# Two post-norms by column chunk, gate rows made ahead of them, and a feed-forward block that begins with its first group

## The reference

```python
def rms_norm_2(x, g):
    y = xf * lax.rsqrt(jnp.mean(xf * xf, axis=-1, keepdims=True) + EPS)
    return (y * g.astype(jnp.float32)).astype(x.dtype)
...
mod = jax.nn.silu(c) @ w_mod[l] + b_mod[l]
sh_m, sc_m, ga_m, sh_f, sc_f, ga_f = [m[:, None, :] for m in jnp.split(mod, N_MOD, axis=-1)]
...
y = gated_merge(y_c, y_h, p_gc, p_gh, w_out[l])
x = x + ga_m * rms_norm_2(y, norm_post_mix[l])
h2 = modulate(rms_norm_2(x, norm_pre_mlp[l]), sh_f, sc_f)
x = x + ga_f * rms_norm_2(sq_relu_mlp(h2, mlp_w1[l], mlp_w2[l]), norm_post_mlp[l])
```

## Time and profile before

| | us |
| --- | --- |
| median of 3 runs | 2971.78 |
| lowest and highest | 2967.68, 2972.05 |
| the profiled execution | 2973.79 |
| span of its trace | 2972.0 |
| PE busy in it | 2857.4 |
| DVE busy | 2014.7 |
| ACT busy | 1355.9 |

### The profile page before, as it was taken

One profiled execution on the slowest core, in us unless ns is written; L12 is line 12 of the kernel. 1 busy time (PEld: TensorE's weight loads), 2 busy tenths in 40 slices (PEclk: granted clock), 3 DMA queues, 4 the chain that ended last, 5 costly groups with the idle time before them and its releaser, 6 DMA issues.

```text
span 2972.0 us, 34985 instructions
## 1 busy us (share of the span) xinstructions
PE 2857.4 (96%) x13258; PEld 2370.4 (80%) x13258; DVE 2014.7 (68%) x2263; ACT 1355.9 (46%) x1633; POOL 146.9 (5%) x103
## 2 busy tenths in 40 slices
PE   7998999999999999999999999989979999999997
PEld 6786787888888887787788888888857888888886
DVE  4665779799789787776686487575557754544554
ACT  4446354444443454555444444653434444344442
POOL 0100001010010100000000000000000001010000
PEclk9999999999999999999999999999989999999998
DMA  7661878987878988555666666405547876665653
GB/s 227 198 195 51 277 255 282 320 266 271 286 258 285 324 287 276 177 184 177 202 184 193 194 188 182 131 1 184 190 144 241 275 220 185 193 189 191 188 188 120
DMA packets 322668, 622.52 MB, mean 209 GB/s; under 512 B 27415, under 2 KB 29591, under 8 KB 320919
## 3 DMA queue, kind: packets, MB, share of 16 engines
q1 hardware_dynamic: 319015, 597.96, 63.1%
q10 hardware_dynamic: 3504, 22.55, 2.0%
HBM read 614.14 MB, written 7.24 MB: 209 GB/s over the span
## 4 chain that ended last, share of the span: by engine, by line
PE 83%; DVE 9%; issue 3%; DMA 3%; ACT 2%; SPq 0%; DVEq 0%; POOL 0%; ACTq 0%; POOLq 0%
PE ps L1281 77%; DVE macc L1930 3%; DVE wlo L1741 2%; DMA raw<-w_in 2%; PE ps L1386 1%; PE ps L1256 1%; ACT whi L648 1%; PE ps L1428 1%; PE ps L1646 1%; DVE tcol L2051 1%; PE ps L1628 1%; PE ps L1608 1%; DMA raw<-w_up 0%; DMA raw<-w_o 0%; PE ps L1357 0%
## 5 line engine op out<-in xcount | busy, mean ns | idle before, releaser
L1741 DVE TENSOR_TENSOR wlo<-raw,whi 128x1024 fp32r<-128x1024 f32 x940 | 1171.9, 1252 | 812.0 <-ACT whi L648 807.5
L648 ACT ACTIVATE whi<-raw 128x1024 fp32r<-128x1024 f32 x940 | 995.8, 1060 | 1312.1 <-PE ps L1281 1222.1
L1281 PE MATMUL ps<-whi,hhi 128*128 128x512 f32 x2064 | 811.7, 393 | 1.7 <-DVE hlo L2057 1.2
L1281 PE MATMUL ps<-whi,hlo 128*128 128x512 f32 x2064 | 804.7, 390 | 0.0
L1281 PE MATMUL ps<-wlo,hhi 128*128 128x512 f32 x2064 | 804.3, 390 | 0.0
L1281 PE MATMUL ps<-whi,xhi 128*128 128x512 f32 x1632 | 649.6, 398 | 21.0 <-DVE wlo L1741 16.4
L1281 PE MATMUL ps<-wlo,xhi 128*128 128x512 f32 x1632 | 642.2, 393 | 0.0
L1281 PE MATMUL ps<-whi,xlo 128*128 128x512 f32 x1632 | 641.8, 393 | 0.0
L1281 PEld LDWEIGHTS ps<-whi,hhi 128*128 128x128 f32 x2064 | 388.2, 188 | 83.4 <-DVE hlo L2057 3.1
L1281 PEld LDWEIGHTS ps<-whi,hlo 128*128 128x128 f32 x2064 | 388.0, 188 | 81.6
L1281 PEld LDWEIGHTS ps<-wlo,hhi 128*128 128x128 f32 x2064 | 388.3, 188 | 79.5 <-issue 1.0
(11 more groups left out here) (280 smaller groups left out, 1548.0 us busy)
## 6 DMA issues: line engine op xcount, KB each, us to landing
raw<-w_in SPq DMA_DIRECT2D x296, 512.0 KB, 4.3
raw<-mlp_w SPq DMA_DIRECT2D x256, 512.0 KB, 3.7
mraw<-w_mod SPq DMA_DIRECT2D x192, 512.0 KB, 6.1
raw<-w_up SPq DMA_DIRECT2D x128, 512.0 KB, 5.1
raw<-w_down SPq DMA_DIRECT2D x128, 512.0 KB, 5.3
raw<-w_o SPq DMA_DIRECT2D x32, 512.0 KB, 5.8
raw<-w_ple_gate SPq DMA_DIRECT2D x32, 512.0 KB, 4.2
raw<-w_out SPq DMA_DIRECT2D x32, 512.0 KB, 4.3
```

The source lines that it names most:

```text
L648: nc.scalar.activation(whi[:, s % NSLOT], raw[:, s % NSLOT], ACT.Copy).then_inc(hi_done, 1)
L1281: ins = nc.tensor.matmul(ps[:, bank(par) + th], a[:, kt, th * P:(th + 1) * P], b[:, (s + u) % NSLOT, k], start=(kt == 0 and m == 0), stop= ...
L1741: nc.vector.tensor_tensor(wlo[:, s % NSLOT], raw[:, s % NSLOT], whi[:, s % NSLOT].bitcast(F32), ALU.subtract)\
```

## The change

- `post3` goes by chunk. ACT squares each chunk of `wo2` out of PSUM instead of copying it, DVE multiplies it by the gate row into `yrow`, and after the last one DVE adds the four chunks to `res` while ACT squares them for `norm4`.
- The gate row of `post3` is made in the stage `pw`, in four parts of 512, in banks 6 and 7; that of `post4` in chunks 18 and 19 of `mlp2`. ACT copies each part out.
- PE begins `mlp2` when the first group is ready; groups 2 to 7 are transposed ahead of pieces 0 to 5 of its first chunk.
- The last part of the modulation work moves from chunks 0 to 7 of `mlp2` to chunks 8 to 15.
- `post4` goes by chunk: three of the four result chunks are squared and multiplied during the chunk after them. SP sends each chunk of `res`, 512 KB, as it is finished.

The core of the diff:

```diff
@@ both @@
-                    ("mlp1", "sbbb", 16, (4,) * 8), ("mlp1", "sssss", 24, (5,) * 8), ("mlp2", "ssss", 0, (4,) * 8)]
+                    ("mlp1", "sbbb", 16, (4,) * 8), ("mlp1", "sssss", 24, (5,) * 8), ("mlp2", "ssss", 8, (4,) * 8)]
@@ SP @@
             mlp("mlp2", w_up2, w_down2)
+            for c in range(4):
+                cs = slice(c * NCH, (c + 1) * NCH)
+                sp.wait_ge(S["res", "post4"], c + 1)
+                sp.dma_start(rows_of(out[0])[:, :, cs], res[:, :, cs]).then_inc(out_done, 16)
+            sp.wait_ge(out_done, 64)
@@ ACT @@
+            def gate_row_out(n, j, dst):
+                act.wait_ge(gb_done, 4 * n + j + 1)
+                nc.scalar.activation(dst[:, j * NCH:(j + 1) * NCH], ps[:, 6 + j % 2], ACT.Copy).then_inc(gb_out, 1)
...
+                        10: lambda: gate_row_out(0, 0, gbc), 11: lambda: gate_row_out(0, 1, gbc),
+                        14: lambda: gate_row_out(0, 2, gbc), 15: lambda: gate_row_out(0, 3, gbc)}
...
-                chunk(p0 + 8 * c, evac_to(yrow, c * NCH, g0 + c), extra=slots(wo_slots, 8 * c))
...
-            postnorm_gated("post3", 0, yrow, lambda e: e.wait_ge(acc_free, plan["mlp2"][1] + 2))
-            norm_mod("norm4", res, lambda e: e.wait_ge(S["res", "post3"], 2))
-            mlp("mlp2", 16, False, {})
-            postnorm_gated("post4", 1, yrow, lambda e: e.wait_ge(acc_free, plan["end"][1] + 2))
-            for th in range(TH):
-                act.wait_ge(S["res", "post4"], 2)
-                act.dma_start(rows_of(out[0])[:, th], res[:, th]).then_inc(out_done, 16)
-            act.wait_ge(out_done, 32)
+                chunk(p0 + 8 * c, lambda c=c, g=g0 + c: psum_squares("post3", c, g), extra=slots(wo_slots, 8 * c))
+            for c in range(4):
+                res_squares("norm4", "post3", ojunk, c)
+            first_row("norm4")
...
+            last = 8 * (len(SEQ) * NSB - 4)
+            mlp("mlp2", 16, False, place({**{g: (lambda g=g: mod_high("norm4", g, xhi)) for g in range(8)},
+                                          **{146 + 4 * j: (lambda j=j: gate_row_out(1, j, gbc4)) for j in range(4)},
+                                          **{last + 8 * c + 10: (lambda c=c: post4_squares(c)) for c in range(3)}}))
+            post4_squares(3)
@@ PE @@
+            def gate_row(n, k, j):
+                pe.wait_ge(mcol_done, k + 1)
+                if n == 0 and j % 2 == 0:
+                    pe.wait_ge(oc_done, NPAIR)
+                if 4 * n + j >= 2:
+                    pe.wait_ge(gb_out, 4 * n + j - 1)
+                for b in range(4):
+                    kt = 4 * j + b
+                    ins = nc.tensor.matmul(ps[:, 6 + j % 2, b * P:(b + 1) * P], mcol[:, k, kt:kt + 1].to_broadcast([P, P]),
+                                           ident, start=True, stop=True)
+                ins.then_inc(gb_done, 1)
...
-            gate_rows(3, plan["mlp2"][1])
-            norm("norm4")
-            pe.wait_ge(x_lo, 24)
-            mlp("mlp2", 16, {})
-            gate_rows(4, plan["end"][1])
+            pe.wait_ge(S["xn", "norm4"], 1)
+            pe.wait_ge(S["xm", "norm4"], 1)
+            norm_turn("norm4", 0, xs)
+            norm_turn("norm4", 1, xs)
+
+            def mlp2_part(u):
+                if u + 2 < 8:
+                    norm_turn("norm4", u + 2, xs)
+                pe.wait_ge(x_lo, 16 + u + 1)
+            mlp("mlp2", 16, place({**{u: (lambda u=u: mlp2_part(u)) for u in range(8)},
+                                   **{144 + 4 * j: (lambda j=j: gate_row(1, 4, j)) for j in range(4)}}))
@@ DVE @@
             for c in range(4):
-                chunk(plan["wo2"][0] + 8 * c, extra=slots(wo_slots, 8 * c))
...
+                chunk(p0 + 8 * c, lambda c=c, g=g0 + c: psum_gain("post3", c, g), extra=slots(wo_slots, 8 * c))
             dve.wait_ge(reload, 16)
-            postnorm("post3", yrow, lambda e: e.wait_ge(acc_free, plan["mlp2"][1] + 2))
-            norm_mod("norm4", res, lambda e: e.wait_ge(S["res", "post3"], 2), mcol[:, 2], modT[:, 3 * KT:4 * KT, 0])
-            mlp("mlp2", {})
+            for c in range(4):
+                dve.wait_ge(acc_free, g0 + c + 3)
+                post_res("post3", yrow, c)
+            chunk_mean_square("norm4", SQ)
+            dve.wait_ge(S["res", "post3"], 4)
+            scaled_row("norm4", res, xs)
...
+            mlp("mlp2", place({0: lambda: [col4(0), col4(1), low4(0)], **{g: (lambda g=g: [col4(g + 1), low4(g)]) for g in range(1, 7)},
+                               7: lambda: low4(7), 137: last_mods, **{last + 8 * c + 13: (lambda c=c: post4_gain(c)) for c in range(3)}}))
+            chunk_mean_square("post4", SS)
+            post4_gain(3)
+            for c in range(4):
+                dve.wait_ge(S["yg", "post4"], c + 1)
+                post_res("post4", yrow, c)
```

More of the change, by code:

```diff
@@ L66 @@
 RMS = {k: n for n, k in enumerate(ROOTS)}
-WHOLE = {k: n for n, k in enumerate(k for k in ROOTS if k not in ("post0", "post2", "norm3"))}
+WHOLE = {k: n for n, k in enumerate(("norm0", "norm1", "normc", "post1", "norm2"))}
 def shape_constants():
@@ L407, in build @@
                 S[w, k] = sem(f"{w}_{k}")
-        for k in ("post0", "post2", "norm3"):
+        for k in ("post0", "post2", "norm3", "post3", "norm4", "post4"):
             S["sq", k] = sem(f"sq_{k}")
@@ L787, in _ @@
             for c in range(4):
[L788 removed]
+                chunk(p0 + 8 * c, lambda c=c, g=g0 + c: psum_squares("post0", c, g), extra={6: p_high} if c == 0 else {})
             gain1 = col("pre_mlp_norm")
@@ L1769, in plain_low @@
                 ins.then_inc(t_free, 1)
-            def postnorm(k, row, wait_row, xs=xs):
-                mean_square(k, row, wait_row, xs)
-                dve.wait_ge(rstd_done, RMS[k] + 1)
-                dve.wait_ge(S["gain", k], 16)
-                for th in range(TH):
-                    nc.vector.scalar_tensor_tensor(out=xs[:, th], in0=row[:, th], scalar=stat[:, 8 + th:9 + th], in1=gbc[:],
-                                                   op0=ALU.mult, op1=ALU.mult).then_inc(S["scaled", k], 1)
-                for th in range(TH):
-                    dve.wait_ge(S["scaled", k], th + 1)
-                    nc.vector.tensor_tensor(res[:, th], res[:, th], xs[:, th], ALU.add).then_inc(S["res", k], 1)
             gain0, n0 = col("pre_mix_norm"), COL["pre_mix_norm"]
@@ L2149, in post2_res @@
             def post2_res(c):
-                dve.wait_ge(rstd_done, RMS["post2"] + 1)
                 dve.wait_ge(S["yg", "post2"], c + 1)
-                cs = slice(c * NCH, (c + 1) * NCH)
-                for th in range(TH):
-                    ins = nc.vector.scalar_tensor_tensor(out=res[:, th, cs], in0=erow[:, th, cs], scalar=stat[:, 8 + th:9 + th],
-                                                         in1=res[:, th, cs], op0=ALU.mult, op1=ALU.add)
-                ins.then_inc(S["res", "post2"], 1)
+                post_res("post2", erow, c)
             gate_slots = {6: lambda: decayed_keys(0), 7: lambda: decayed_keys(1),
@@ L2367, in _ @@
             wo_slots = {1: lambda: y_low(4), 2: lambda: y_low(5), 4: lambda: y_low(6), 5: lambda: y_low(7)}
+            p0, g0 = plan["wo2"]
             for c in range(4):
[L2369 to L2379 removed]
@@ new lines, in _, with last_mods, post4_gain @@
+            low4 = lambda g: mod_low("norm4", g, xhi, xlo)
+            def last_mods():
+                dve.wait_ge(m_red, N_MCH)
+                step(nc.vector.tensor_tensor(modT[:, NM:, 0], mps[:, NM:, 0], bmod[:, NM:], ALU.add))
+                nc.vector.tensor_tensor(mcol[:, 4], modT[:, NM:, 0], col("norm_post_mlp_2"), ALU.mult).then_inc(mcol_done, 1)
+            def post4_gain(c):
+                dve.wait_ge(S["sq", "post4"], c + 1)
+                dve.wait_ge(gb_out, 8)
+                cs = slice(c * NCH, (c + 1) * NCH)
+                nc.vector.tensor_tensor(yrow[:, :, cs], yrow[:, :, cs], gbc4[:, cs].unsqueeze(1).to_broadcast([P, TH, NCH]), ALU.mult)\
+                    .then_inc(S["yg", "post4"], 1)
```

125 lines of the change are left out of this document (48 added, 77 removed).

## The result

| | us |
| --- | --- |
| changed kernel, median of 4 runs | 2952.36 (2946.78 to 2954.33) |
| kernel before, median of 4 runs | 2969.73 (2966.61 to 2972.05) |
| ratio, with its 95% interval | 0.9938 (0.9923 to 0.9954) |
| profiled execution, changed and before | 2946.78 and 2973.79 |
| span of its trace, changed and before | 2945.0 and 2972.0 |

The change makes the kernel 0.62% faster, 17.4 us between the medians. The forecast was 2955 us, and the range 2949 to 2962. It was made from a median of 2971.78 for the kernel before, which came out at 2969.73 beside the changed kernel: 2.05 of the 2.6 us between forecast and result are this base.

What follows compares the result with a forecast made beforehand. PE, busy 96% of the span, was taken as the bound, with 59.7 us of standstill and end to shorten. Terms -19.6 + 5.0 + 7.7 - 9.8 = -16.7 us gave 2955 us, range 2949 to 2962.

Steps and rivals of the forecast that it cites:

- standstill ahead of `mlp2`: From the last matmul of `wo2` to the first of `mlp2`: 16.7 us against 36.3, 19.6 saved.
- first 11 pieces: First chunk of `mlp2`, now with six more groups of transposes: 37.1 us against 32.05, 5.0 lost.
- gate rows: Small matmuls moved into `pw` and `mlp2`, both in PE's way: 2 x 3.85 = 7.7 us lost.
- chunks of `wo2`, modulation work: PSUM banks freed later in `wo2`, and modulation work in later `mlp2` chunks: both 0; the latter at most 4.2 us.
- end: Behind the last matmul, `post4` by chunk and 512 KB transfers: 13.6 us against 23.4, 9.8 saved.
- rival 6: `norm4` squares wait for one another and end late: at most 1 us taken back; counted within the forecast's 0.79.
- 23.45 for six: Time from first to seventh piece in `x2`, taken over for the interleaved first chunk of `mlp2`; its total was 37.1 us.
- rival 3: Bank waits and the four-chunk chain stretch PE's pauses in `wo2`: 2967 us, no change; chance 0.06.
- rival 2: DVE becomes late in `mlp2` through the moved modulation work: up to 4.2 us, 2959; chance 0.06.
- Rival 5: The 512 KB transfers at the end take 6.1 us each instead of 3.2: 2958 us; chance 0.05.
- Rival 1: Clock stays low into `mlp2`: gain gone after 6.4 more pieces, 2994 us if for two chunks; chance 0.04.
- Rival 4: Interleaving in the first chunk of `mlp2` nearly free, gate rows at 7.0: 2952 us; counted within the forecast's 0.79.

Runs made afterwards that it cites:

- e1: Changed kernel with PE waiting for all eight groups of `norm4` before the first matmul of `mlp2`; 2961.61 us, ratio 0.9964 to the kernel before.
- e11: Changed kernel with `post3` and the squares of `norm4` on whole rows again, group start and early gate row kept; 2954.3 us in one run.
- e7: Changed kernel with 50 unused small matmuls keeping PE busy in the standstill ahead of `mlp2`; 2952.31 us in one run.
- e9: Changed kernel with e8's reorderings and e7's 50 unused matmuls together; 2945.19 us, ratio 0.9911 to the kernel before.
- e2: Changed kernel with every small matmul of both gate rows issued twice, results unchanged; 2959.09 us, ratio 0.9963 to the kernel before.
- e3: Changed kernel with gate rows made by transposes instead of matmuls with the identity; 2949.97 us, ratio 0.9926 to the kernel before.
- e8: Changed kernel with transposed gate rows, DVE's low parts before the next group's modulation, last `post4` product in its own buffer; 2946.84 us, ratio 0.9922 to before.
- e5: Changed kernel with the last modulation work back in chunks 0 to 7 of `mlp2`; 2958.52 us in one run.
- e6: Changed kernel with the output in two transfers of 1 MB instead of four of 512 KB; 2948.13 us in one run.

## Why the prediction was right, and which term was off

The likeliest case happened, and the terms of its sum held, one apart:

| term | forecast | measured |
| --- | --- | --- |
| standstill ahead of `mlp2` | -19.6 | -19.45 |
| first 11 pieces | **+5.0** | **+2.9** |
| gate rows | +7.7 | +7.1 |
| chunks of `wo2`, modulation work | 0 | +0.4 |
| end | -9.8 | -9.75 |
| sum | -16.7 | -18.8 |

**The standstill** was built from six steps of the first block, 16.7 us. In the changed kernel they are, from the same chain and timelines: 2.8 to the first addition (2191.17 to 2193.98), 5.4 for the additions, 1.7 to the reduction (2199.36 to 2201.06), 1.1 to the root's end, 2.1 to the first transpose, 3.7 to the first matmul. That makes 16.8. Only the squares left over are off, 1.7 for 1.4: they start one chunk behind and at 1.40 us a chunk lose a little more. This is all that there was to rival 6. e1 and e11 show that it really is the two named causes that bring the gain.

**The first chunk is the mis-sized term.** The step "23.45 for six" took the row of `x2` whole, and its first piece ran at 1.2 GHz (5.50 us in the earlier trace rows). The changed kernel's first piece took 3.03. The pause of a piece was read rightly. In the chain, the first piece of one pair starts at 2207.99 and that of the next at 2214.99:

```profile
2213.34 0.99 DVE tcol L2046 x2
2214.33 0.61 DVE xlo L2052
...
2214.99 3.07 PE ps L1283 x12
...
2229.01 13.90 PE ps L1283 x60
```

That is 7.0 us for two pieces, and 21.0 from 2207.99 to 2229.01 for six, 3.5 each, by way of the split, the modulation of the next group, and only then `xlo`. Six of these and five free pieces of 2.75 give 34.8, which is the 34.77 measured. What I priced wrongly is the clock, which I took as late when it can be early. The runs give its price. A late return costs half of the time by which it is late, on top of the full-clock time. That is 34.77 for the changed order (e7), 30.0 without groups in the chunk, and 33.1 for the reordered one (taken from e9 itself, so its row is no test):

| kernel | back | full-clock time + half | measured |
| --- | --- | --- | --- |
| before | +4.0 | 30.0 + 2.0 = 32.0 | 31.89 |
| e1 | +5.3 | 30.0 + 2.6 = 32.6 | 32.55 |
| e2 | +2.2 | 34.77 + 1.1 = 35.9 | 35.76 |
| e3 | +4.5 | 34.77 + 2.3 = 37.0 | 36.86 |
| e8 | +4.9 | 33.1 + 2.4 = 35.5 | 35.50 |
| e9 | +5.1 | 33.1 + 2.5 = 35.6 | 35.47 |

It comes out within 0.2 us. With the clock 4.5 us late, as in e3, the term would have been 36.86 - 31.89 = +5.0, which is the forecast. The price of interleaving itself is 34.77 - 30.0 = 4.8 us, of which e8's order gives 1.6 back.

**The gate rows** cost 8 x 0.89 = 7.1 us. The forecast took the row of the old place (3.85 for four parts) for both. In the stretches that the chain shows as PE alone they cost what a record costs. The forecast's lower bound, 7.0, was the better reading. e2 and e3 show that it scales both ways.

**The chunks of `wo2`** did not make PE wait: behind the gate rows `pw` to `wo2` holds 0.08 us more than before, so rival 3 is out. The forecast said against it that stage `o` shows no pause at a boundary. That holds in the trace of before for the boundaries at 344.4 and 366.6 us, but not for the first, at 311.9: there DVE is late with modulation work, the product stands on the chain (318.16, 1.14 us), and PE waits 1.37 and then 1.91 us for splits. `wo2` has no such work. **The modulation work** in its new place costs at most 0.35 us, so rival 2 is out; its upper bound of 4.2 was far too wide. e5 adds that leaving it would have cost only some 0.6.

**The end** came out by its steps: 13.7 us for 13.6. The slow root was there (1.61), the additions took 5.39, and the last 512 KB landed in 2.9 instead of 3.2. Rival 5 is out, and e6 shows the other side of it.

**Rival 1**, the clock that stays low, did not happen in any of the 12 traces. The latest return was 5.3 us after the first matmul (e1), 5.1 with groups in the first chunk (e9), and the pauses between the pieces did not let the clock fall again. Rival 4 had the right time (2952) for a wrong reason: interleaving is not free, it was the clock that was kind.

## What to carry to other kernels

When a cost is taken over from a like stage, split it into its time at full clock and what the clock adds. The first says what the order costs, and the second differs from run to run and belongs in the range. In a loop where PE waits for the low part of the next tile, put what PE waits for ahead of what it needs only a piece later (3.5 to 3.2 us a piece here, at no cost that the traces show). A serial norm between two matmul stages shrinks by chunks and by starting on the first group, but what is moved under the matmuls is paid in full on a PE that is busy 96% of the time, so make it in its cheapest form first (0.44 instead of 0.89 us).
